# Six split weight halves instead of three in the expert stage of a decoder trunk

## The reference

```python
def moe_swiglu(h, router_w, w_gu, w_down):      # 8 experts, FF_EXPERT = 3584
    logits = (xf @ router_w).astype(jnp.float32)
    top_v, top_i = lax.top_k(logits, TOP_K)     # TOP_K = 2
    gates = jax.nn.softmax(top_v, axis=-1)
    cw = jnp.sum(jax.nn.one_hot(top_i, N_EXPERTS, dtype=jnp.float32) * gates[..., None], axis=1)
    ...
    for e in range(N_EXPERTS):
        out = out + cw[:, e:e + 1] * swiglu(xf, w_gu[e], w_down[e])
```

## Time and profile before

| what | us |
|---|---|
| three runs, median (lowest to highest) | 1798.68 (1798.62 to 1800.74) |
| the profiled execution | 1800.64 |
| its span, first to last instruction | 1798.4 |
| mixer, dense stage and second mixer, to 783 us of the span | 783 |
| routing and block 0, to the gather for block 1 | 151 |
| blocks 1 to 7 and the final norm | 865 |

### The profile page before, as it was taken

How to read it: one execution, slowest core, us unless ns; L and a number is a source line. 1 busy time by engine, 2 the same in 40 slices (tenths; PEclk the granted TensorE clock), 3 DMA queues, 4 the chain that set the end, 5 groups by cost and what they waited for, 6 DMA issues and landing times.

```text
span 1798.4 us, 22701 instructions
## 1 busy us (share of the span) xinstructions
PE 1688.0 (94%) x7843; PEld 1367.7 (76%) x7843; DVE 1320.4 (73%) x1156; ACT 1123.9 (62%) x1120; POOL 184.0 (10%) x400
## 2 busy tenths in 40 slices
PE   6999999999979999969998999999999989999896
PEld 4888887888768888857886778877788767788674
DVE  4457756544454676666888988879998889888896
ACT  4456744443345657335767877768867778777784
POOL 1033331000000344134000000000000000000000
PEclk8999999999989999968998999989999999999998
DMA  6644454555535445543988999979999889899793
GB/s 267 249 169 168 167 184 153 190 185 188 183 119 185 161 164 180 185 171 136 375 341 317 420 377 355 374 277 405 410 345 374 335 353 421 345 374 378 304 418 156
DMA packets 71778, 488.29 MB, mean 272 GB/s; under 512 B 8668, under 2 KB 11949, under 8 KB 13229
## 3 DMA queue, kind: packets, MB, share of 16 engines
q1 hardware_dynamic: 69052, 483.89, 70.2%
q10 hardware_dynamic: 2672, 3.70, 0.6%
HBM read 484.94 MB, written 2.62 MB: 271 GB/s over the span
## 4 chain that ended last, share of the span: by engine, by line
PE 76%; DVE 10%; issue 6%; ACT 5%; POOL 1%; DMA 0%; DVEq 0%; SPq 0%; ACTq 0%; POOLq 0%
PE bank L360 20%; PE bank L362 20%; PE bank L361 20%; DVE w_lo L355 7%; ACT w_hi L350 4%; PE bank L1679 4%; PE bank L1680 3%; PE bank L1694 2%; PE bank L1661 1%; PE bank L1523 1%; PE bank L1685 1%; POOL q_buf L644 1%; DVE cT_hi L1314 1%; PE bank L1539 0%; DVE nw L1012 0%
## 5 line engine op out<-in xcount | busy, mean ns | idle before, releaser
L355 DVE TENSOR_TENSOR w_lo<-w_raw,w_hi 128x2048 fp32r<-128x2048 f32 x450 | 1023.2, 2293 | 344.0 <-ACT w_hi L350 343.8
L350 ACT ACTIVATE w_hi<-w_raw 128x2048 fp32r<-128x2048 f32 x454 | 868.7, 1916 | 462.5 <-PE bank L362 415.4
L360 PE MATMUL bank<-w_hi,hT_hi 128*128 128x512 f32 x1200 | 480.9, 401 | 11.7 <-DVE hT_lo L1037 8.9
L362 PE MATMUL bank<-w_hi,hT_lo 128*128 128x512 f32 x1200 | 472.0, 393 | 0.0
L361 PE MATMUL bank<-w_lo,hT_hi 128*128 128x512 f32 x1200 | 471.0, 393 | 0.0
L360 PEld LDWEIGHTS bank<-w_hi,hT_hi 128*128 128x128 f32 x1200 | 228.1, 190 | 63.4 <-DVE hT_lo L1037 10.8
L362 PEld LDWEIGHTS bank<-w_hi,hT_lo 128*128 128x128 f32 x1200 | 227.6, 190 | 49.5
L361 PEld LDWEIGHTS bank<-w_lo,hT_hi 128*128 128x128 f32 x1200 | 228.4, 190 | 45.3
L1679 PE MATMUL bank<-w_hi,hT_hi 128*128 128x512 f32 x448 | 186.4, 416 | 23.7 <-DVE w_lo L355 23.5
L1680 PE MATMUL bank<-w_lo,hT_hi 128*128 128x512 f32 x448 | 180.0, 402 | 0.0
L360 PE MATMUL bank<-w_hi,cT_hi 128*128 128x512 f32 x376 | 147.1, 391 | 1.5 <-DVE cT_lo L1181 1.5
(11 more groups left out here) (267 smaller groups left out, 1387.3 us busy)
## 6 DMA issues: line engine op xcount, KB each, us to landing
w_raw<-expert_slabs SPq DMA_DIRECT2D x333, 1024.0 KB, 5.3
w_raw<-mix_slabs SPq DMA_DIRECT2D x88, 1024.0 KB, 4.7
w_raw<-dense_slabs SPq DMA_DIRECT2D x33, 1024.0 KB, 4.8
bias_lines<-bias ACTq DMA_DIRECT2D x2, 768.0 KB, 4.6
X<-in_x SPq DMA_DIRECT2D x2, 512.0 KB, 4.2
bias<-bias_lines SPq DMA_DIRECT2D x1, 1024.0 KB, 7.1
yT<-in_ffn_norm_g ACTq DMA_DIRECT2D x2, 512.0 KB, 5.9
v_buf<-expert_slabs SPq DMA_DIRECT2D x1, 1024.0 KB, 4.8
```

Of the source, the lines that this page charges most:

```text
L350: act.activation(w_hi[:, n % SPLIT, :], early_raw[n] if early else w_raw[:, n % RAW, :], ACT.Copy).then_inc(hi_ready, 1)
L355: eng.tensor_tensor(w_lo[:, n % SPLIT, :], early_raw[n] if early else w_raw[:, n % RAW, :], w_hi[:, n % SPLIT, :], ALU.subtract).then_inc( ...
L360: pe.matmul(dst, hi, whi, start=first, stop=False, skip_group_check=True)
L362: return pe.matmul(dst, lo, whi, start=False, stop=last, skip_group_check=True)
```

## The change

In the expert stage the split parts get six slots each instead of three, `n % 6`. The new ones lie where buffers of the mixers are idle by then: `e_q`, `e_k`, `e_v`, `e_bias` and `e_uy` are names for the space of `q_buf`, `k_buf`, `v_buf`, `bias`, and of `uT` with `yT`; one high slot is the unused second half of `hT_hi` and `hT_lo`, now one tensor `hT`, so that this half is written and read as two stretches of 1024 (`in_pair`). `split_hi` waits for half n-6 to be used instead of n-3, but for the first ones in the opening, which wait for the buffer's last reader (`hi_slot_free`).

The engines' programs move with it. ScalarE and VectorE run a step ahead: in loop step m they split the halves that TensorE uses in the step after, and by the end of a block they have split the first four halves of the next. `silu`, `take_gate`, the turns, `take_y`, `add_scattered`, `spread_out` and `next_pick` take new places among the splits; the first loop step is written out (`m1`). TensorE takes the first gate half of step 1 before the first turn, the three first scatter products after its second half, the fourth after the up halves. The clearing matmuls go: the first product of a block into banks 4 and 5 starts them. In the opening one half less is loaded ahead, and half `MOE0 + 3` is split inside the routing, on VectorE between `pick_r` and the operations that lead to `fold_ready`. GpSimd's `terms` has a smaller place (`wgtT`), so the products with `col_no` are made in three rounds of two rows instead of one of six: 36 small products, 12 additions and 4 copies instead of 12, 4 and 2. The final gain has a buffer of its own. The mixers and the dense stage keep their three slots and their order.

```diff
-        hT_hi = sb("hT_hi", [P, KC * SEQ], F32R)
-        hT_lo = sb("hT_lo", [P, KC * SEQ], F32R)
-        q_buf = sb("q_buf", [P, KC * SEQ])
-        k_buf = sb("k_buf", [P, KC * SEQ])
-        v_buf = sb("v_buf", [P, KC * SEQ])
+        hT = sb("hT", [P, 2, KC * SEQ], F32R)
...
+        with ExitStack() as trunk:
+            def shared(name, shape):
+                return trunk.enter_context(nc.sbuf_tensor(name, shape, F32))
+
+            q_buf = shared("q_buf", [P, KC * SEQ])
+            k_buf = shared("k_buf", [P, KC * SEQ])
+            v_buf = shared("v_buf", [P, KC * SEQ])
+            bias = shared("bias", [P, HEADS, LINE])
+            uT = shared("uT", [P, 4, SEQ + 2])
+            yT = shared("yT", [P, KC * P])
+
+        e_q, e_k, e_v, e_bias = (sb(name, [P, HALF], F32R) for name in ("e_q", "e_k", "e_v", "e_bias"))
+        last_gain = sb("last_gain", [P, D])
+        e_uy = sb("e_uy", [P, 2 * 4 * (SEQ + 2)], F32R)
...
-        early_raw = {MOE0 + RAW // 2: v_buf[:, :],
-                     MOE0 + RAW // 2 + 1: bias[:, :, :].rearrange("p h j -> p (h j)")[:, 0:HALF],
-                     MOE0 + RAW // 2 + 2: k_buf[:, :]}
+        early_raw = {MOE0 + 3: v_buf[:, :], MOE0 + 4: bias_flat[:, 0:HALF]}
+
+        moe_hi = {0: w_hi[:, 0, :], 1: w_hi[:, 1, :], 2: w_hi[:, 2, :], 3: e_k[:, :],
+                  4: hT[:, :, KC * P:2 * KC * P], 5: e_q[:, :]}
+        moe_lo = {0: w_lo[:, 0, :], 1: w_lo[:, 1, :], 2: w_lo[:, 2, :], 3: e_uy[:, 0:HALF],
+                  4: e_v[:, :], 5: e_bias[:, :]}
...
+        def hi_slot_free(act, n, cyc, opening):
+
+            if n < MOE0 or opening and n < MOE0 + 2:
+                if n >= SPLIT:
+                    act.wait_ge(half_used, n - SPLIT + 1 + RAW * cyc)
+            elif opening and n == MOE0 + 2:
+                job_in_bank(act, DEPTH - 1, ("turn_m", 1), 7)
+            elif opening and n == MOE0 + 3:
+                act.wait_ge(logits_ps, TT)
+            elif opening and n == MOE0 + 4:
+                act.wait_ge(hr_lo_ready, TT)
+            else:
+                act.wait_ge(half_used, n - RAW + 1 + RAW * cyc)
...
+            hi_slot_free(act, n, cyc, opening)
+            if n >= MOE0 and n % RAW == 4:
+                act.activation(hi_slot(n), in_pair(raw_of(n, early)),
+                               ACT.Copy).then_inc(hi_ready, 1)
+            else:
+                act.activation(hi_slot(n), raw_of(n, early), ACT.Copy).then_inc(hi_ready, 1)
...
-                    job_in_bank(sp, 1, ("turn_m", 1), 7)
-                    load_early(sp, MOE0 + 5, gate_up(1, 1))
-                    for i in range(2, 4):
+                    for i in range(1, 4):
                         load_half(sp, MOE0 + 4 + i, gate_up(i, 1))
                     load_half(sp, MOE0 + 8, down_rows(0, 0))
                     load_half(sp, MOE0 + 9, down_rows(1, 0), slot_free=True)
-                    for i in range(2):
-                        load_half(sp, MOE0 + 10 + i, gate_up(i, 2), slot_free=True)
+                    load_half(sp, MOE0 + 10, gate_up(0, 2), slot_free=True)
+                    load_half(sp, MOE0 + 11, gate_up(1, 2))
...
-            for c in range(COLS):
-                chain(pool.tensor_tensor(terms[:, :, c, :], src[:, :, :],
-                                         col_no[:, c:c + 1, :].to_broadcast([P, 6, 2 * EXPERTS]), ALU.mult))
-            for n in (8, 4, 2, 1):
-                chain(pool.tensor_tensor(terms[:, :, :, 0:n], terms[:, :, :, 0:n], terms[:, :, :, n:2 * n], ALU.add))
-            chain(pool.tensor_copy(seats[:, :, 1:COLS], terms[:, 1:6, 1:COLS, 0]))
-            chain(pool.tensor_copy(ctl[:, 1:1 + COLS], terms[:, 0, :, 0]))
+            for r in (0, 2, 4):
+                for c in range(COLS):
+                    chain(pool.tensor_tensor(terms[:, :, c, :], src[:, r:r + 2, :],
+                                             col_no[:, c:c + 1, :].to_broadcast([P, 2, 2 * EXPERTS]), ALU.mult))
+                for n in (8, 4, 2, 1):
+                    chain(pool.tensor_tensor(terms[:, :, :, 0:n], terms[:, :, :, 0:n], terms[:, :, :, n:2 * n], ALU.add))
+                if r:
+                    chain(pool.tensor_copy(seats[:, r - 1:r + 1, 1:COLS], terms[:, :, 1:COLS, 0]))
+                else:
+                    chain(pool.tensor_copy(ctl[:, 1:1 + COLS], terms[:, 0, :, 0]))
+                    chain(pool.tensor_copy(seats[:, 0:1, 1:COLS], terms[:, 1:2, 1:COLS, 0]))
...
+                split_hi(act, MOE0 + 3)
...
-                def begin(b, opening=False):
+                def begin(b):
                     c = CYCLES * b
-                    if not opening:
-                        split_hi(act, MOE0, c)
-                        split_hi(act, MOE0 + 1, c)
-                        take_y(b)
-                        split_hi(act, MOE0 + 2, c)
+                    split_hi(act, MOE0 + 4, c)
+                    take_y(b)
+                    split_hi(act, MOE0 + 5, c)
...
+                def wide_silu(b, m):
+                    act.wait_ge(half_used, MOE0 + 2 + RAW * (CYCLES * b + m))
+                    silu(b, m)
...
+                    def step(m, m1=False):
+                        cm = c + m
+                        for i in (4, 5, 6):
                             split_hi(act, MOE0 + i, cm)
-                        act.wait_ge(half_used, MOE0 + 8 + RAW * cm)
-                        silu(b, m)
-                        split_hi(act, MOE0 + 11, cm)
-                    turn_hi(b, MSTEPS - 1)
+                        wide_silu(b, m)
+                        for i in (7, 8):
+                            split_hi(act, MOE0 + i, cm)
+                        if m1:
+                            spread_out(b)
+                        split_hi(act, MOE0 + 9, cm)
+                        turn_hi(b, m)
...
+                    def step(m, m1=False, ahead=True):
+                        cm = c + m
+                        split_hi(act, MOE0 + 4, cm)
+                        if m1:
+                            fold_silu(b, 0)
+                        else:
+                            fold_hi(i2, m - 1)
+                        split_hi(act, MOE0 + 5, cm)
+                        if m1:
+                            fold_hi(i2, 0)
+                        take_gate(b, m, MOE0 + RAW * cm)
+                        if ahead:
+                            split_hi(act, MOE0 + 6, cm)
+                        take_up(MOE0 + 2 + RAW * cm)
+                        if ahead:
+                            split_hi(act, MOE0 + 7, cm)
+                            split_hi(act, MOE0 + 8, cm)
+                        if m1:
+                            spread_out(b)
+                        if ahead:
+                            split_hi(act, MOE0 + 9, cm)
+                        fold_silu(b, m)
...
+                    if closing:
+                        with act.Fori(2, MSTEPS - 1) as m:
+                            step(m)
+                        step(MSTEPS - 1, ahead=False)
...
+                split_lo(dve, MOE0 + 3)
...
+                    def step(m, m1=False):
+                        cm = c + m
+                        split_lo(dve, MOE0 + 4, cm)
+                        split_lo(dve, MOE0 + 5, cm)
+                        if m1 and not opening:
+                            for i in range(3):
+                                add_scattered(b, i)
                         split_lo(dve, MOE0 + 6, cm)
-                        turn_lo(b, m - 1)
-                        for i in range(7, 11):
-                            split_lo(dve, MOE0 + i, cm)
                         gated(b, m)
-                        split_lo(dve, MOE0 + 11, cm)
-                    turn_lo(b, MSTEPS - 1)
+                        split_lo(dve, MOE0 + 7, cm)
+                        if m1 and not opening:
+                            add_scattered(b, 3)
+                        split_lo(dve, MOE0 + 8, cm)
+                        if m1:
+                            next_pick(b)
+                        split_lo(dve, MOE0 + 9, cm)
+                        turn_lo(b, m)
...
+                    def step(m, m1=False, ahead=True):
+                        cm = c + m
+                        split_lo(dve, MOE0 + 4, cm)
+                        if m1:
+                            fold_prod(b, i2, 0)
+                        else:
+                            fold_lo(b, m - 1)
+                        split_lo(dve, MOE0 + 5, cm)
+                        if m1:
+                            fold_lo(b, 0)
+                            for i in range(3):
+                                add_scattered(b, i)
+                        if ahead:
+                            for i in (6, 7):
+                                split_lo(dve, MOE0 + i, cm)
+                        if m1:
+                            add_scattered(b, 3)
+                        if ahead:
+                            split_lo(dve, MOE0 + 8, cm)
+                        if m1 and not closing:
```

(18 more changed lines are left out.)

192 lines of the change are left out of this document (100 added, 92 removed).

## The result

The changed kernel takes 1785.0 us (median of 4 runs, 1783.07 to 1788.46) where the kernel before takes 1799.71 (4 runs, 1798.62 to 1800.92): ratio 0.9918, 95% interval 0.9905 to 0.9932. That is 14.7 us faster. The forecast was 1770, 28.3 us faster; the direction and the range held, the gain came to half.

What follows compares the result with a forecast made beforehand. It took TensorE to bound wide blocks and, in narrow ones, the three-slot ring and late block starts. Terms -11.0 - 11.0 - 8.7 - 8.1 + 4.8 + 5.7 = -28.3 us gave 1770 us, range 1757 to 1787.

Steps and rivals of the forecast that it cites:

- the term of the wide blocks: Blocks 2, 4 and 6: TensorE stays the bound; net +1.6 us each, +4.8 in all.
- the new wait at the front: Wide block's front: down rows queue behind five VectorE splits between two fold_lo operations; 3.1 us.
- the clock: TensorE's granted clock falling to 1.2 GHz at new waits, named as a sign of being wrong; no size in the sum.
- the savings: Wide blocks: two clearing matmuls gone, 0.5 us, and short waits in the first four halves gone, 1.7 us.
- Narrow blocks: Blocks 1, 3 and 5: VectorE's work sets 107.5 us from gather to gather; savings 11.0, 11.0 and 8.7.
- the ring of three slots: Narrow step: copy, subtraction and product run partly in turn, giving 14.82 us; forecast 13.9 a step after the change.
- DMA as a rival: Loads bind the narrow steps: narrow blocks take 111.1 us, total 1785; chance 0.18.
- Block 7: Last block: fold of step 6 starts 105.6 us after the gather against 113.7; 8.1 us saved.
- The opening: Routing and block 0: first gather 4.1 us later, TensorE waits 5 us for GpSimd's chain, less savings; +5.7.
- The chain's end: Opening: GpSimd's longer chain, started about 821, has route_ready at 861.5.
- the savings put at 3.4: Opening: three halves not copied behind TensorE, no first-turn wait, no clearing, no 1.1 us wait behind next_pick; 3.4 us.
- The split in two stretches: Rival: copy or subtraction on the hT slot costs more; at double time total 1834; chance 0.07.

Runs made afterwards that it cites:

- a_fill: Changed kernel with zero filler matmuls in TensorE's two waits at the ends of blocks 1, 3 and 5: 1780.88 us, ratio 0.9890.
- b_nozero: Kernel before without its two clearing matmuls a block, step 1 written out ahead of the loop: 1801.87 us, ratio 1.0012.
- a_order2: Changed kernel with two instead of four of the next block's halves split ahead at the ends of blocks 1, 3, 5: 1770.46 us, ratio 0.9833.
- a_oldorder: Changed kernel's six slots, opening and GpSimd rounds, with the kernel before's block order and clearing matmuls: 1791.08 us, ratio 0.9957.
- b_halfload: Kernel before with expert loads halved, dense-stage loops hit too, so one wide block more ran: 1925.60 us, only block lengths comparable.
- a_halfload2: Changed kernel with loads halved in the expert stage alone, output not the reference's: 1777.46 us, ratio 0.9880.
- a_terms6: Changed kernel with GpSimd's routing chain in one round of six rows instead of three of two: 1780.68 us, ratio 0.9893.
- a_order3: Changed kernel with three instead of four of the next block's halves split ahead at narrow ends: 1779.93 us, ratio 0.9882.
- a_order0: Changed kernel with none of the next block's halves split ahead at the ends of blocks 1, 3, 5: 1780.88 us, ratio 0.9903.
- a_best: Changed kernel with the moves of a_order2 and a_terms6, plus VectorE's split of half MOE0 + 3 behind the routing: 1761.44 us, ratio 0.9782.

## Why the prediction was half right

**The step that failed** is the term of the wide blocks, "Net +1.6 each". Its parts: the new wait at the front was put at 3.1 us and is 2.02 + 1.14 = 3.2 in block 2 (3.0 and 3.6 in blocks 4 and 6). Its whole length is set by the very five subtractions that the prediction named; that ScalarE's evacuation is late too, and splits the wait in two, it had not seen. Two parts were wrong. The first is the clock, which the prediction mentions only among what would make it wrong, with no number in the sum: the last down rows run at 1.2 GHz behind these waits, for 4.0 us in block 2, 3.2 in block 4 and 4.4 in block 6. At 0.43 us a matmul instead of 0.23 that costs 1.9, 1.5 and 2.1 us, and `a_fill` gives 1.9 back in block 2. The gather's last quarter loses 0.7 us more to the clock. The second is the savings, put at 0.5 for clearing and 1.7 for short waits, less 0.7 for the fifth half (measured 0.84). `b_nozero` shows that clearing was free; and with waits and clock both gone, in `a_order2`, a wide block is only 0.3 us shorter than before, not 1.5. The trace of `a_order2` closes the sum. There the down rows start 3.6 us behind the gather, here 7.8, which is 4.2 more for the wait and the slow quarter; against that, `a_order2` waits 0.6 at the first turn, and this kernel doesn't. Thus 4.2 + 1.9 - 0.6 - 0.3 = 5.2 where 5.1 were measured, and 4.8 and 5.4 in blocks 4 and 6 where 4.7 and 5.3 were.

**The larger mistake** was one of choice, not of size: 3.2 us of wait had been seen and taken as the price of having halves ready. `a_order2` shows that it buys nothing: VectorE idles 5.29 us right after it, so two of the four halves can be split there.

**Narrow blocks** (forecast 107.5, measured 108.6, 107.3, 108.6): right, by the right mechanism. The step is VectorE's six subtractions and two fold operations, 13.9, and `a_oldorder` shows that the ring of three slots was what held 14.82. The rest is the loads, 0.6 to 0.7 us, which lengthen the last loop step (14.49 us in block 1), and the clock: blocks 1 and 5 have a mean of 0.98 and take 1.3 us more than block 3, which has 1.00. The dips follow TensorE's wait for `turn_lo` before the wide block's last down rows, 0.97 and 1.05 us there; block 3 has one of 1.04 us with no dip behind it:

```profile
946.46 0.79 PE L410 MATMUL bank<-e_q,cT_hi 128*128 128x512 f32 x1 [0.97 <-DVE cT_lo L1395]
...
1184.34 0.49 PE L410 MATMUL bank<-e_q,cT_hi 128*128 128x512 f32 x1 [1.04 <-DVE cT_lo L1395]
```

**DMA as a rival.** Its total, 1785, was met exactly, and by another road: `b_halfload` and `a_halfload2` show that the loads bound nothing before, and after it cost 0.6 to 0.7 us a narrow block instead of 3.6. A total that agrees is no evidence for a mechanism. ScalarE's waits do end with DMA, which the prediction named as a sign that would refute it; they turned out small in this kernel.

**Block 7** (105.6 forecast, 105.4 measured) was right in part by luck. The count holds neither late loads nor the clock; with both out of the way, in `a_halfload2`, the block takes 103.5. So the count was 2.1 us too long, and 1.9 us of loads and clock made up for it.

**The opening** (+5.7 forecast, +8.2 measured): the first gather was right (4.1 and 4.16 later). The chain's end was right too (861.5 against 861.93), but partly by luck: GpSimd's products (L699) begin at 824.5, not at 821, and from there it takes 37.4 us, not 40.5. TensorE's loss behind `next_pick` came to 4.18 us of wait and a slow stretch (the next matmul takes 0.79 us), 6.8 in all by `a_terms6`, not 5. That leaves 2.8 us for the savings put at 3.4, which contained the clearing. The rule of the Trainium skill ("SBUF — State Buffer", "Who interferes with whom") agrees with the trace in kind: in 846.4 to 847.1 GpSimd's operations take 0.25 us during the product with its PSUM input and 2.41 us as soon as a subtraction with two SBUF inputs begins. Whether it saved the 2 us on the chain, the end of the chain can't tell, since the late start hides as much.

**The split in two stretches** costs the same (L403 2.28 beside L406 2.28 to 2.29); that rival falls.

**Late loads, where the rest has become faster.** A narrow block or block 7 behind a shortened wide block is sometimes 2 to 3 us longer (block 5 in `a_order2` 110.6, clock 0.97; block 7 in `a_terms6` and `a_order3`). The traces show two parts. In block 5 of `a_order2` ScalarE's copies wait for loads, and the time between TensorE's first down rows of two steps, 13.9 us until then, becomes 14.9; at half the bytes, in `a_halfload2`, it stays at 13.9 to the end of the block. And behind the longer wait the clock falls for 3.1 us, which by the spacings above is an estimated 1.5 us.

```profile
1499.94 1.92 ACT L397 ACTIVATE e_k<-w_raw 128x2048 fp32r<-128x2048 f32 x1 [0.64 <-DMA w_raw<-expert_slabs]
...
1494.78 0.49 PE L1814 MATMUL bank<-e_k,cT_hi 128*128 128x512 f32 x1 [0.88 <-DVE cT_hi L1406]
...
1509.68 0.78 PE L1814 MATMUL bank<-e_k,cT_hi 128*128 128x512 f32 x1 [1.91 <-DVE cT_hi L1406]
```

This block has two such falls, at 1410.93 and here. The same block in `a_order0` has a last step of 14.7 us, no fall, and takes 107.4, 3.3 us less. So the prediction's DMA rival, wrong for this change, is what the next gains meet.

**Still open:** when a wait brings the clock down. In `a_best` a wait as long as that of the last row above, in the same place of block 1, has none behind it, and no run holds the clock up inside a narrow block:

```profile
1035.31 0.49 PE L1810 MATMUL bank<-e_k,cT_hi 128*128 128x512 f32 x1 [1.90 <-DVE cT_hi L1402]
```

## What to carry to other kernels

More buffers let an engine work ahead, but its queue is in order: ask what is queued behind each piece of work done ahead, and place no more of it than TensorE's cover can carry. The best of the counts tried was in the middle (two of four). Price a wait of TensorE not only by its length but by the matmuls behind it; and look for the idle stretch that follows a stall, as that is where the work belongs. Work taken off TensorE where it waits anyway, like the clearing matmuls, brings nothing.
